# Window-buffer copies moved to SP's queue between its weight loads, in 2 KB rows, and key and value stores moved from ACT to SP

## The reference

```python
mod = silu(c) @ w_ada + b_ada                       # 6 x 1024 columns
proj = (rmsnorm(x) * (1 + sc1) + sh1) @ w_in        # q, k, v of mixers A and B, forget gates
# mixer A: forgetting attention, B: dilated window attention (with rotary)
# samples: A over 2048 cached rows in 16 pages, B over a window buffer of 2048 rows
x = x + gt1 * (concat(rmsnorm(oa), rmsnorm(ob)) @ w_o)
h2 = rmsnorm(x) * (1 + sc2) + sh2
x = x + gt2 * (routed_top8_of_64_experts(h2) + shared_expert(h2))
# _dilated_decode, per sample: the updated window buffer is an output
ek = jnp.concatenate([buf_k, k_new], axis=1); return ..., ek[:, Sd:], ev[:, Sd:]
```

## Time and profile before

| what | value |
|---|---|
| median of 3 runs | 1534.81 us (1532.04 to 1537.07) |
| profiled execution, own time | 1547.54 us |
| its span | 1545.9 us |
| PE busy | 1286.9 us (83%) |
| DVE, ACT, POOL busy | 488.7, 267.0, 250.4 us |
| moved by DMA | 461.85 MB in 165148 packets, mean 299 GB/s |
| HBM read, written | 431.89 MB, 106.07 MB |
| mean granted clock of PE | 0.909 |

### The profile page before, as it was taken

How to read it: one execution, slowest core, us unless ns; L and a number is a source line. 1 busy time by engine, 2 the same in 40 slices (tenths; PEclk the granted TensorE clock), 3 DMA queues, 4 the chain that set the end, 5 groups by cost and what they waited for, 6 DMA issues and landing times.

```text
span 1545.9 us, 17562 instructions
## 1 busy us (share of the span) xinstructions
PE 1286.9 (83%) x5908; PEld 656.2 (42%) x5908; DVE 488.7 (32%) x1400; ACT 267.0 (17%) x599; POOL 250.4 (16%) x294
## 2 busy tenths in 40 slices
PE   4966979957777888878589999999899899899880
PEld 2754756424443434444234444444344344344330
DVE  2352455114433423225242222322122222122213
ACT  2221111104322225111001111111011111111110
POOL 1200000022323210000001222222122122122110
PEclk9987989988978788988799999999999999999995
DMA  9999995189989659467627999999999999999964
GB/s 360 390 337 356 389 333 190 68 262 334 387 295 382 218 209 346 150 222 247 239 70 242 334 341 358 365 360 362 351 364 335 357 347 346 347 338 345 348 202 124
DMA packets 165148, 461.85 MB, mean 299 GB/s; under 512 B 13233, under 2 KB 14513, under 8 KB 163905
## 3 DMA queue, kind: packets, MB, share of 16 engines
q1 hardware_dynamic: 129472, 294.96, 52.2%
q0 software_dynamic: 29376, 131.02, 27.3%
q10 hardware_dynamic: 6208, 34.72, 6.6%
HBM read 431.89 MB, written 106.07 MB: 348 GB/s over the span
## 4 chain that ended last, share of the span: by engine, by line
PE 63%; DMA 19%; DVE 5%; issue 5%; ACT 3%; SPq 3%; ACTq 2%; POOL 0%; POOLq 0%; DVEq 0%
PE banks L679 20%; PE banks L703 11%; DMA reg_w<-in_w_ada 7%; PE banks L1492 5%; PE banks L535 5%; PE banks L1482 4%; DMA routed_sum<-reg_w,sidx 3%; DMA reg_w<-h_rows,gidx 3%; DMA reg_w<-in_ws_down 2%; PE banks L1622 2%; DMA reg_q<-in_cache_k 2%; PE banks L1664 1%; PE banks L580 1%; PE banks L601 1%; PE banks L666 1%
## 5 line engine op out<-in xcount | busy, mean ns | idle before, releaser
L679 PE MATMUL banks<-reg_q,reg_w 128*128 128x512 f32 (+1 forms) x768 | 310.8, 622 | 18.7 <-issue 15.4
L679 PEld LDWEIGHTS banks<-reg_q,reg_w 128*128 128x128 f32 (+1 forms) x768 | 120.9, 176 | 182.9 <-issue 180.4
L703 PE MATMUL banks<-reg_q,reg_w 128*128 128x512 f32 (+1 forms) x384 | 154.8, 603 | 8.6 <-ACT reg_w L1197 8.6
L1296 POOL DMA_INDIRECT routed_sum<-reg_w,sidx x64 | 97.6, 1526 | 305.8 <-DMA routed_sum<-reg_w,sidx 147.3
L1053 DVE SCALAR_TENSOR_TENSOR reg_w<-banks,small,reg_w 128x256 f32<-128x256 f32 x52 | 25.1, 483 | 340.8 <-ACT reg_w L1192 340.8
L1292 POOL DMA_INDIRECT reg_w<-h_rows,gidx x52 | 55.4, 1065 | 476.5 <-DVE gidx L1013 445.3
L679 PE MATMUL banks<-hT,reg_w 128*128 128x512 f32 (+1 forms) x256 | 120.5, 626 | 10.8 <-issue 10.8
L1192 ACT ACTIVATE reg_w<-banks 128x256 f32<-128x256 f32 x52 | 20.0, 385 | 462.8 <-PE banks L679 462.8
L1492 PE MATMUL banks<-hT,reg_q 128*128 128x260 f32 x384 | 90.2, 395 | 2.4 <-DVE hT L1748 1.6
L1065 DVE COPY reg_w<-banks 128x512 f32<-128x512 f32 x52 | 36.0, 691 | 163.2 <-PE banks L703 163.2
L703 PEld LDWEIGHTS banks<-reg_q,reg_w 128*128 128x128 f32 (+1 forms) x384 | 55.5, 170 | 70.2 <-issue 58.5
(11 more groups left out here) (373 smaller groups left out, 1479.2 us busy)
## 6 DMA issues: line engine op xcount, KB each, us to landing
reg_q<-in_w_gate_up SPq DMA_DIRECT2D x48, 2048.0 KB, 20.9
reg_q<-in_w_down SPq DMA_DIRECT2D x48, 1024.0 KB, 21.8
hT<-in_w_gate_up SPq DMA_DIRECT2D x16, 2048.0 KB
out_win_k_s<-in_win_k POOLq DMA_DIRECT2D x8, 4094.0 KB, 19.6
out_win_v_s<-in_win_v ACTq DMA_DIRECT2D x6, 4094.0 KB, 15.5
reg_w<-in_w_ada SPq DMA_DIRECT2D x11, 2048.0 KB, 24.1
reg_w<-in_w_down SPq DMA_DIRECT2D x16, 1024.0 KB, 23.3
reg_q<-in_cache_k POOLq DMA_DIRECT2D x32, 256.0 KB, 6.3
```

What stands on the lines that cost most here:

```text
L679: last = mm(pb[j % 2][of, :], lhsT=xT[:, j % 2, k, of], rhs=wgu[LOAD[p] % 4][:, k, :], start=(k == 0), stop=(k == KC - 1))
L703: last = mm(pb[6 + hh][of, :], lhsT=aT[:, j % 2, c, of], rhs=wdn[LOAD[p] % 4][:, c, hh * 512:hh * 512 + 512], start=(c == 0), stop=(c == 1))
L1296: nc.gpsimd.indirect_dma_start(rsum, bass.IndirectOffsetOnAxis(ap=idx[0:of.stop - of.start, :], axis=0), y[of, u, :], None, bounds_check=T ...
```

## The change

Twelve copies, not ten, are asked for before the attention, by SP and not by POOL: one behind each load of `GROUPS` from ada 4 to ada 11. Four, not six, are left to ACT in the output projection: one at each of t = 1 to 4, where it was one at t = 0 to 3 and two at t = 4. Each copy goes in rows of 512 floats, with an outer count of 89 and an inner one of 23. The 15 stores go from ACT, ahead of its exponentials, to SP, ahead of its load of item 4. SP's end waits for the twelve copies, which POOL did.

```diff
-NLATE = 6
+NLATE = 4
...
             sp.wait_ge(r_out, 16 * TT)
+            sp.wait_ge(win_out, 16 * (2 * NS - NLATE))
             sp.wait_ge(late_out, 16 * NLATE)
...
-            pool.wait_ge(win_out, 16 * (2 * NS - NLATE))
...
             name, out, b = ("win_k", "win_k_s", n) if n < NS else ("win_v", "win_v_s", n - NS)
-            rows = (PAST - 1) * W
-            engine.dma_start(
-                O[out][b, 0:PAST - 1, :].rearrange("r c -> (r c)").rearrange("(a n) -> a n", n=rows // 16),
-                I[name][b, 1:PAST, :].rearrange("r c -> (r c)").rearrange("(a n) -> a n", n=rows // 16)
-            ).then_inc(done, 16)
+            engine.dma_start(O[out][b, 0:PAST - 1, :].rearrange("(a r) c -> r a c", a=23),
+                             I[name][b, 1:PAST, :].rearrange("(a r) c -> r a c", a=23)).then_inc(done, 16)
...
+        def put_out(sp):
+
+            sp.wait_ge(rope_set, 2 * NP)
+            sp.wait_ge(knew_set, 1)
+            sp.wait_ge(raw_taken, NTAKEN)
+            for m, (ko, vo) in enumerate((("k_a_p", "v_a_p"), ("win_k_p", "win_v_p"))):
+                sp.dma_start(O[ko], qkT[:, (2 * m + 1) * NP:(2 * m + 2) * NP, 0:SEQ]).then_inc(kv_out, 16)
+                for t in range(QB):
+                    sp.dma_start(O[vo][t * P:t * P + P, :], v[:, t, m * W:m * W + W]).then_inc(kv_out, 16)
+            sp.dma_start(O["k_a_s"], qkT[:, NP:2 * NP, SEQ:T]).then_inc(kv_out, 16)
+            sp.dma_start(O["v_a_s"], v[0:NS, QB, 0:W]).then_inc(kv_out, 16)
+            sp.dma_start(O["win_k_s"][:, PAST - 1, :], knew).then_inc(kv_out, 16)
+            sp.dma_start(O["win_v_s"][:, PAST - 1, :], v[0:NS, QB, W:2 * W]).then_inc(kv_out, 16)
+            sp.dma_start(O["lf"], lfs[:, :]).then_inc(kv_out, 16)
...
                 sp.dma_start(wslot[b], I["w_" + which][:, at:at + 512].rearrange("(k p) n -> p k n", p=P)
                              ).then_inc(group_in[b], 16)
+                if GROUPS.index((which, n, b)) >= len(GROUPS) - 1 - (2 * NS - NLATE) and (which, n, b) != GROUPS[-1]:
+                    copy_window(sp, GROUPS.index((which, n, b)) - (len(GROUPS) - 1 - (2 * NS - NLATE)), win_out)
...
             for i in range(len(ITEMS)):
+                if i == RING:
+                    put_out(sp)
...
-            for n in range(2 * NS - NLATE):
-                pool.wait_ge(raw_ready, AT["qk", 0] + 2 + n * 22 // (2 * NS - NLATE))
-                copy_window(pool, n, win_out)
...
             load_decay(0)
-            act.wait_ge(rope_set, 2 * NP)
-            act.wait_ge(knew_set, 1)
-            act.wait_ge(raw_taken, NTAKEN)
...
             act.wait_ge(cols_set, 1)
```

## The result

| | before | after |
|---|---|---|
| median of the runs on one chip | 1535.6 us (1532.04 to 1537.07, 4 runs) | 3861.39 us (3858.69 to 3868.41, 4 runs) |
| ratio, 95% interval | | 2.515 [2.507, 2.522] |
| profiled execution, span | 1547.54, 1545.9 us | 3859.55, 3857.9 us |
| PE busy | 1286.9 us | 1293.7 us |
| mean granted clock of PE | 0.909 | 0.667 |

What follows compares the result with a forecast made beforehand. Projections were taken as DMA-bound to 230 us, then PE-bound to 322; attention and experts near full on both. Terms 1886 - 10 + 623 - 17 = +2482 us on 1547.5, less 12.7, gave about 4020 us, range 3750 to 4450.

Steps and rivals of the forecast that it cites:

- How a copy is shared out: All copies: the outermost count alone sets the DMA engines used, so prime 89 gives one engine for 4.19 MB; chance 0.85.
- The row's price: Copies on one engine: 84 ns per 2 KB row, so 172 us a copy, where it was 15.5 us.
- the end at 96 ns: Upper end of the price per 2 KB row, from ACT's whole queue: 403 us more, 4420 us in all.
- SP held, PE idle: Projections: twelve copies between SP's weight loads delay the last load to 2174 us and the stage's end to 2208; +1886 us.
- The stores: Attention's start: 15 stores moved to SP let ACT's first exponential come earlier; -10 us, ends 0 and -20.
- ACT held in each of its four issues: Output projection: ACT stands at each of its four copies until the rest is gone, 677 us instead of 54; +623 us.
- The 128 rows that were thought to fit: ACT's queue, output projection: some 128 rows of a copy fit the engine's queue, 10.8 us of work.
- ws_down: After the output projection: PE's 16.6 us wait for this load goes, with two copies fewer there; -17 us.
- The experts: Last stage, some 700 us with PE and DMA near full: no added time predicted, 0 us.
- rival 3: Output projection: ACT isn't held at its four copies, which compete with the experts' loads instead; 3956 us, chance 0.02.
- Rival 1: All copies: spread over 16 engines, 11.5 us each; 1513 us, chance 0.09 faster and 0.02 for about the same time.
- rival 2: All copies: one engine each, but another each time, and a queue that holds neither SP nor ACT; 1862 us, chance 0.02.

Runs made afterwards that it cites:

- e4: Kernel before the change with only the 15 stores moved from ACT to SP; 1530.58 us, 1.000 of the unchanged kernel.
- e5: Changed kernel with 89 x 23 rows only in ACT's four late copies, the twelve early ones in old rows; 2065.76 us, 1.351 of the unchanged kernel.
- e6: Changed kernel with 89 x 23 rows only in SP's twelve early copies, the four late ones in old rows; 3327.56 us, 2.171 of the unchanged kernel.
- e2: Changed kernel with all copies in their old 64 rows of 65,504 bytes; 1529.38 us, 1.000 of the unchanged kernel.
- e1: Changed kernel with each copy as 16 x 127 rows of 2 KB and a rest of 15 rows; 1548.34 us, 1.012 of the unchanged kernel.
- e11: Changed kernel with each copy as 16 x 127 rows and the rest of 15 rows left out; 1535.58 us, 0.999 of the unchanged kernel.

## Why the prediction was right, and where not

- **How a copy is shared out: right.** The count of closing packets, by which one engine was forecast, holds for the copies themselves (4 left of 11,120 on ACT's queue, and SP's count fits with one for each of its twelve) and for 12 and 16 outermost.
- **The row's price: right within 5%.** 84 ns was taken, 80.1 and 80.6 measured; the end at 96 ns, taken from whole queues, was far off. Twelve copies and loads at 169.0 instead of 177.4 us are 101 us less. 83 us of them show in the landing of the last load; of the other 18, 11 lie in the first two pairs, which took 178.0 and 171.1 us, and 7 stay open.
- **SP held, PE idle: right in size.** The issue that stands is the load behind the copy, not "at the copy's line". PE waits before the ada groups, 312 to 317 us four times and 147 to 149 three times, not "some 170 us at a time"; the sum is the same. What follows the last load took 35 us, 34 were expected.
- **The stores: wrong.** The step took ACT's 30 us of issues as part of the chain; in e4 PE waits 13.3 us less for ACT and 10.9 more for a ring item, and the time is that of before.
- **ACT held in each of its four issues: wrong.** "ACT then stands in each issue until the rest is gone" had the wrong transfer. A copy is taken at once, and the next transfer stands. Three copies and not four lie on ACT's path: 443 us, not 623. The 128 rows that were thought to fit rested on a third of SP's first loads having been moved in 13.00 us. At the 364 GB/s of the earlier trace rows it was up to three quarters. By an estimate from the copies' times, 3 x 165.0 + 9.1 - 498.6, the room was 5.5 us, some 70 rows, where 10.8 us were taken.
- **ws_down: right.** No wait for it is left (it was asked for at 2790.77 us, ahead of ACT's last stand of 169 us), the routing is 22 us shorter; 17 were taken.
- **The experts were costed at nothing: wrong.** The fourth copy, which was thought to be over, ran beside them and cost 93 us (e5, with it, 818 us of experts; e6, without, 721). It was in rival 3, with all four copies; with one it is true.
- **Two readings were loose**, and neither is in the sum. "Nearly idle to 310" holds from 270 us on; the slice before it shows five tenths. Attention had "both near full": PE was busy 199 of 268 us and the DMA engines at 0.84.

The sum was 2482, the difference of the profiled executions 2312. The errors are -82 + 3 - 180 - 5 + 93 = -171 us (the rest is rounding); the experts took half back of what ACT's free last copy saved. That the time came within 4% of the forecast is in part luck: a term that was 180 us too long and one that was left out hide each other. The direction and the factor rested on one term, the outer count, and that was read from a line of packet counts. Rival 1 is refuted by the packets and by e2 and e1; rival 2 by the issues of 134 to 174 us, since it needed a queue that holds neither SP nor ACT. Whether each copy rode the same engine no row tells; SP's 169.0 us and ACT's 165.0 agree best on a price if the copy and the 64 rows of the load are on one engine: 80.1 and 80.6 ns, against 82.6 for the copy alone.

## What to carry to other kernels

Before a copy is reshaped, look at its outermost count: 89 x 23 rows and 16 x 127 rows are the same bytes in the same 2 KB rows, and with the first the whole kernel takes 2.5 times as long as with the second. A queue's packets less the rows of its transfers give the number of engines that took part, and show such a copy at once. Where large copies that nobody waits for share the engines with loads that somebody does, their place in these runs is behind the loads, in the stretch where the engines were idle, and not too many of them: eight between late loads and four behind the last gained 3.1%, six behind the last gained 1% less.

## What was not expected of the hardware

- **An issue stands for its predecessor.** A copy of 2,047 rows for one engine is taken in 0.79 us on ACT and 3.6 to 7.4 us on SP; the next transfer on the same queue stands 134 to 174 us. e1 shows it with 0.61 and 15.18 us. So the last large transfer of a row of them is free for the engine that asks, and the work behind the one before pays.
- **One engine slows all.** While one copy was left on one engine, the DMA engines moved 228 GB/s in the experts' stage, against 333 once it was over, and PE was busy for 60% (119 of 200 us), against 91% (454 of 500). In e6, with no such copy left there, the experts' loads run at 337 GB/s.
- **Two transfers instead of one** cost 1.3% of the kernel (1.012 for e1 against 0.999 for e11), though they moved the same bytes but for 0.7% of the copies.
